# The first adaLN product moves from VectorE to TensorE in a hybrid decoder layer

## The chip, the cores and the metric

The kernel runs on one core of one Trainium2 chip. The metric is the device time of one execution, in microseconds (us). TensorE does the matrix products, VectorE (DVE in the rows) and ScalarE (ACT) the elementwise work, GpSimd (POOL) some more of it, and SyncE (SP) issues most transfers.

## The reference, cut to what matters

A decoder layer for 512 tokens of width 1024, one sequence. All data are fp32.

```python
c_act = silu(c)                                   # 1024 values
ada = c_act @ w_ada + b_ada                       # 1024 x 6144, split in six
sh_a, sc_a, g_a, sh_f, sc_f, g_f = split(ada, 6)
h = rmsnorm(x, norm_mix_w) * (1 + sc_a) + sh_a
proj = h @ w_in                                   # gq, gk, gv, gg, glr, hq, hf, hi, hg, ma, mb
log_alpha = log_sigmoid(glr @ w_gk2 + b_gk2) / 16 # glr has 16 columns
h_res = x + g_a * token_mixer(...)                # two gated linear attentions, merged, @ w_out
h = rmsnorm(h_res, norm_ffn_w) * (1 + sc_f) + sh_f
h_res = h_res + g_f * conv_ffn(h)                 # w_up, causal conv of 3, silu gate, w_down
out = rmsnorm(h_res, final_norm_w)
```

The change is about the first lines: `sh_a` and `sc_a` (columns 0 to 2047 of `w_ada`), `h`, and the 16 columns `glr`.

## The kernel before

The engines' programs are written out by hand, each engine has one list of instructions in order, and semaphores tie them together; there is no planner. Activations lie transposed in SBUF, features on partitions: eight tiles (KT = 8) of 128 x 512 tokens. Every large product is made of three products of split operands: `h_hi`, `h_lo` and `w_hi`, `w_lo` (the value rounded to a narrower fp32 form and the rest), so `three` (lines 1161 to 1168) issues hi x hi, lo x hi and hi x lo, each with 512 moving columns. Weights come as units of 128 columns x 1024 rows (512 KB) into three `raw` buffers; ScalarE makes `w_hi` (`split_hi`, L514), VectorE `w_lo` (`split_lo`, L785), in a ring of six slots.

The stages are: the start (about 0 to 38 us), the V stage (38 to 72 us), four groups of the mixer (to about 660 us with the output projection), the up and down products of the FFN, and the end. The change touches the first two.

The start. ScalarE issues the load of `x_tok` (L525); SyncE issues eleven small loads of vectors into `rows` (L326), then the weight unit 0, which holds the 16 low rank columns, and the first half of the ada weights in eight tiles with units 1 to 4 between them (L343, L351). TensorE turns `rows` (L1179) and then `x_tok` (L1186, 32 transposes in two halves; the second half waits until ScalarE and VectorE have copied the first out of PSUM as `xT`). ScalarE squares x (L534), VectorE and ScalarE make the inverse root (L851, L853, L541), VectorE spreads it over a diagonal (L860), TensorE sums that with ones (L1191), and ScalarE copies the result as `rb` (L546). GpSimd multiplies `xT` by `rb` into `xn` (L442).

The first ada product (L816, L819) is elementwise: for each tile k of 128 rows of `w_ada`, VectorE adds `ada_w0[k] * c_act[k]` to `ada_acc0` (128 x 1024), and TensorE then sums over partitions with eight products with a column of ones (`ada0_sums`, L1199). This happens in two halves q: half 0 serves the tiles k = 0 to 3 of h, half 1 the tiles 4 to 7. Half 1's eight VectorE steps stand between the `h_rest` steps (L838) in VectorE's list, after `rows_after` of 1, 2, 2 and 3. `ada0_finish` (L827, L830) adds the bias and forms the scale `a_mix`. ScalarE makes `h_hi` (L551) and the full `h_tmp` (L555) from `xn`, VectorE the rest `h_lo` (L838).

The V stage (the loop behind `ada0_sums(0)` in TensorE's list) runs over k = 0 to 7. For each k it does three products for the low rank unit into PSUM bank 2, and three for each of four token tiles t (the columns of units 1 to 4): 15 products per k, 120 in all. `ada0_sums(1)` stands at k = 3, before t = 1. After the stage come the low rank product z (L1289) and the further units, five microseconds or so each.

## Time and profile before

| what | us |
|---|---|
| median of the runs (lowest, highest) | 977.07 (976.78, 978.61) |
| span of the profiled execution | 976.7 |
| TensorE busy in it | 927.2 |
| VectorE busy | 544.0 |
| ScalarE busy | 466.6 |
| GpSimd busy | 179.8 |

The profiled execution's span is 0.4 us below the median of the runs. Times in a row are microseconds from the start of the span, durations in the group rows are busy microseconds and mean nanoseconds of one instruction, and PEld is TensorE's load of a stationary operand, which overlaps its products. The span was one stretch of TensorE work after a start of 38 us in which TensorE mostly waited.

### The profile page before, as it was taken

The numbers are of one execution on the slowest core, as the hardware profiler recorded it, in microseconds if no ns is written. First come the engines' busy times: TensorE is split into PE (matmuls) and PEld (weight loads), VectorE is DVE, ScalarE is ACT, GpSimd is POOL, SyncE is SP. The second block draws the span as 40 slices with busy tenths as digits, with TensorE's granted clock in tenths as the row PEclk, the third lists the DMA queues.
The fourth block names the chain that finished last, engine by engine and source line by source line (L and its number), as shares of the span: only waits on it lengthen the run. The fifth ranks groups of instructions, "written<-read, shape, count | busy, mean of one in ns | idle before, by whom it ended". The sixth has DMA issues, their size and how long they took to land.

```text
span 976.7 us, 13391 instructions
## 1 busy us (share of the span) xinstructions
PE 927.2 (95%) x4759; PEld 763.1 (78%) x4759; DVE 544.0 (56%) x674; ACT 466.6 (48%) x627; POOL 179.8 (18%) x115
## 2 busy tenths in 40 slices
PE   3699999999999999999999898999999999999995
PEld 2578888788887888878888776888888888888884
DVE  4846883567625677256773645664545454634317
ACT  5347664466634667356672743443333333523214
POOL 1501150311403114131041300021221122100002
PEclk9699999999999999999999999999999999999998
DMA  8915542454323543235422162243333333232202
GB/s 291 383 43 178 168 128 67 129 153 108 92 83 110 169 107 86 86 93 177 116 86 64 52 185 65 59 136 105 88 104 89 102 92 104 88 132 88 84 0 87
DMA packets 144238, 111.74 MB, mean 114 GB/s; under 512 B 3376, under 2 KB 131647, under 8 KB 143951
## 3 DMA queue, kind: packets, MB, share of 16 engines
q1 hardware_dynamic: 143647, 109.20, 36.7%
q10 hardware_dynamic: 528, 2.10, 0.6%
q8 instruction: 19, 0.31, 0.1%
q14 instruction: 12, 0.10, 0.0%
q0 software_dynamic: 32, 0.03, 0.0%
HBM read 107.13 MB, written 4.19 MB: 114 GB/s over the span
## 4 chain that ended last, share of the span: by engine, by line
PE 88%; DVE 5%; ACT 3%; issue 2%; DMA 1%; SPq 1%; DVEq 0%; ACTq 0%
PE ps L1165 27%; PE ps L1166 26%; PE ps L1167 26%; PE ps L1271 2%; DVE ada_acc L819 2%; PE ps L1256 2%; PE ps L1267 2%; DMA ada_w<-in_w_ada_dram 1%; DVE hres_tok L1146 1%; DVE w_lo L785 1%; PE ps L1281 1%; PE ps L1243 1%; PE ps L1199 1%; PE ps L1229 1%; ACT L595 1%
## 5 line engine op out<-in xcount | busy, mean ns | idle before, releaser
L1165 PE MATMUL ps<-h_hi,w_hi 128*128 128x512 f32 x872 | 348.4, 399 | 11.5 <-DVE h_lo L838 4.6
L1167 PE MATMUL ps<-h_hi,w_lo 128*128 128x512 f32 x872 | 341.2, 391 | 0.0
L1166 PE MATMUL ps<-h_lo,w_hi 128*128 128x512 f32 x872 | 341.0, 391 | 0.0
L785 DVE TENSOR_TENSOR w_lo<-raw,w_hi 128x1024 fp32r<-128x1024 f32 x147 | 200.0, 1366 | 91.9 <-ACT w_hi L514 91.5
L1165 PEld LDWEIGHTS ps<-h_hi,w_hi 128*128 128x128 f32 x872 | 164.6, 189 | 51.1 <-issue 14.2
L1167 PEld LDWEIGHTS ps<-h_hi,w_lo 128*128 128x128 f32 x872 | 164.6, 189 | 34.9
L1166 PEld LDWEIGHTS ps<-h_lo,w_hi 128*128 128x128 f32 x872 | 164.7, 189 | 34.3 <-issue 1.9
L514 ACT ACTIVATE w_hi<-raw 128x1024 fp32r<-128x1024 f32 x147 | 153.6, 1052 | 73.2 <-PE ps L1167 48.8
L1165 PE MATMUL ps<-w_hi,h_hi 128*128 128x512 f32 x296 | 116.8, 394 | 2.7 <-DVE w_lo L785 2.7
L1166 PE MATMUL ps<-w_lo,h_hi 128*128 128x512 f32 x296 | 116.0, 392 | 0.0
L1167 PE MATMUL ps<-w_hi,h_lo 128*128 128x512 f32 x296 | 115.9, 392 | 0.0
L721 ACT ACTIVATE conv<-ps,vecs 128x512 f32<-128x512 f32 x42 | 32.6, 778 | 130.6 <-PE ps L1167 130.6
L1096 DVE SCALAR_TENSOR_TENSOR conv<-ps,vecs,conv 128x511 f32<-128x511 f32 x44 | 33.0, 749 | 104.3 <-ACT conv L721 99.7
L496 POOL TENSOR_TENSOR prod<-conv 128x512 f32 x21 | 43.3, 2063 | 241.6 <-DVE conv L1100 241.6
L1165 PEld LDWEIGHTS ps<-w_hi,h_hi 128*128 128x128 f32 x296 | 56.1, 190 | 19.1 <-issue 5.1
L1166 PEld LDWEIGHTS ps<-w_lo,h_hi 128*128 128x128 f32 x296 | 56.1, 190 | 11.6
L1167 PEld LDWEIGHTS ps<-w_hi,h_lo 128*128 128x128 f32 x296 | 56.0, 189 | 11.7
L451 POOL TENSOR_TENSOR qs<-qs,qry 128x512 f32<-128x512 f32 x12 | 18.5, 1544 | 207.1 <-ACT qs L575 207.1
L949 DVE SCALAR_TENSOR_TENSOR ada_acc<-ada_w,cols,ada_acc 128x1024 f32<-128x1024 f32 x28 | 36.9, 1316 | 9.0 <-DMA ada_w<-in_w_ada_dram 8.9
L464 POOL TENSOR_TENSOR gate<-gate,oe 128x512 f32<-128x512 f32 x16 | 24.4, 1533 | 85.1 <-DVE oe L956 85.1
L641 ACT ACTIVATE gate<-ps 128x512 f32<-128x512 f32 x16 | 9.6, 597 | 61.8 <-PE ps L1167 61.7
L459 POOL TENSOR_TENSOR gate<-gate,gmul 128x512 f32<-128x512 f32 x16 | 24.4, 1523 | 79.1 <-ACT gmul L645 79.1
(183 smaller groups left out, 936.1 us busy)
## 6 DMA issues: line engine op xcount, KB each, us to landing
raw<-in_w_in_dram SPq DMA_DIRECT2D x73, 512.0 KB, 4.5
ada_w<-in_w_ada_dram SPq DMA_DIRECT2D x48, 512.0 KB, 5.0
...
x_tok<-in_x_dram ACTq DMA_DIRECT2D x1, 2048.0 KB, 8.4
xT_saved_dram<-xT SPq DMA_DIRECT2D x1, 2048.0 KB, 14.2
hres<-xT_saved_dram SPq DMA_DIRECT2D x1, 2048.0 KB, 7.9
```

The lines of the kernel that those rows point to most:

```text
L459: pool.tensor_tensor(gate[:, w], gate[:, w], gmul[:], ALU.mult).then_inc(gated, 1)
L464: pool.tensor_tensor(gate[:, w], gate[:, w], oe[:, w % 2], ALU.mult).then_inc(y_made, 1)
L496: pool.tensor_tensor(prod[:, bass.ds(r * 3 + q, 1), :].rearrange("p a t -> p (a t)"), conv[:, 2 * q], conv[:, 2 * q + 1], ALU.mult).then_i ...
L514: act.activation(w_hi[:, slot(u)].rearrange("p k c -> p (k c)"), raw[:, raw_slot(u)].rearrange("p k c -> p (k c)"), ACT.Copy).then_inc(hi_ ...
L721: act.activation(conv[:, m], ps[:, m], ACT.Identity, bias=vecs[:, bass.ds(ch + V_CONVB, 1)], scale=vecs[:, bass.ds(ch + V_TAP2, 1)]).then_ ...
L785: dve.tensor_tensor(w_lo[:, slot(u)].rearrange("p k c -> p (k c)"), raw[:, raw_slot(u)].rearrange("p k c -> p (k c)"), w_hi[:, slot(u)].re ...
L819: ins = dve.scalar_tensor_tensor(out=ada_acc0[:, q], in0=ada_w0[:, k], scalar=c_act[:, k:k + 1], in1=ada_acc0[:, q], op0=ALU.mult, op1=ALU ...
L949: ins = dve.scalar_tensor_tensor(out=ada_acc[:], in0=ada_w[:, m % 2], scalar=c_act[:, m:m + 1], in1=ada_acc[:], op0=ALU.mult, op1=ALU.add)
L1096: dve.scalar_tensor_tensor(out=conv[:, m, 1:T], in0=ps[:, m, 0:T - 1], scalar=vecs[:, bass.ds(ch + V_TAP1, 1)], in1=conv[:, m, 1:T], op0=A ...
L1165: pe.matmul(dst, a_hi, b_hi, start=start and i == 0, stop=False)
L1166: pe.matmul(dst, a_hi, b_lo, start=False, stop=False)
L1167: last = pe.matmul(dst, a_lo, b_hi, start=False, stop=stop and i == n - 1)
```

## The change

- The first ada product goes to TensorE. `c_act` is repeated 32 times (`c_rep`, 128 x 8 x 32) and is the stationary operand; blocks of 128 columns of `w_ada` are the moving one. The output of block j goes to partitions 32j to 32j + 31 of PSUM bank 7, so up to four blocks (two of shift, two of scale) are in the array at once, in four column groups. It is in plain fp32.
- The weights come in five pieces (`PIECES`: blocks 0-1, 2-3, 4-5, 6, 7, each for shift and scale) into two buffers. Piece 0 is summed before the V stage, pieces 1 to 4 inside it (`SUMS_AFTER`). ScalarE copies each sum out (`ada0_take`), TensorE transposes it into bank 3 (`ada0_turn`, `TURN_AFTER`), VectorE finishes it.
- The sixteen VectorE steps over `ada_w0` are gone. VectorE now makes `xs = xT * a_mix * rb` in one step per tile, and GpSimd's eight steps for `xn` are gone. ScalarE adds the shift, twice (`h_hi`, `h_full`); `h_full` has all eight tiles.
- The low rank projection leaves the list of split units (U_MIX is 0 instead of 1, so slots and counts move by one). GpSimd loads its 16 columns into a zeroed `w_lr` of 32 columns, and TensorE does eight fp32 products with 512 moving columns, in four column groups, just before k = 7, t = 0. The four partial sums stay on four groups of partitions, and z (L1289) sums them through a `gk2_g` that holds `w_gk2` four times.
- SyncE loads c and then x first. ScalarE issues the ten other vector loads. c is transposed apart from the rest.
- The waits for `xT_out` on ScalarE, VectorE and SyncE go; GpSimd's `merge` has one instead. Loads of the later ada pieces wait for `ada0_summed` on SyncE.

```diff
+PIECES = ((0, 2), (2, 2), (4, 2), (6, 1), (7, 1))
+PIECE_BUF = ((0, 0), (1, 0), (0, 0), (1, 0), (1, 1))
+SUMS_AFTER = {(0, 1): 1, (1, 2): 2, (3, 0): 3, (4, 0): 4}
+TURN_AFTER = {(0, 2): 1, (1, 3): 2, (3, 1): 3, (4, 1): 4}
+PIECE_OF = (0, 0, 1, 1, 2, 2, 3, 4)
...
-        ada_w0 = si("ada_w0", [P, KT, D])
-        ada_acc0 = si("ada_acc0", [P, 2, D])
-        h_tmp = si("h_tmp", [P, 2, T])
...
+        xs = si("xs", [P, 2, T])
+        ada_w0 = si("ada_w0", [P, 2, KT, 2, 2 * P])
+        ada_row = si("ada_row", [P, P])
+        h_full = si("h_full", [P, KT, T])
...
-            sp.wait_ge(rows_zero, 1)
-            def row(dst, src, n):
-                sp.dma_start(rows[dst % P:dst % P + n, dst // P, :], src).then_inc(rows_in, 16)
-            row(V_C, c[0].rearrange("(r p) -> r p", p=P), 8)
...
-            row(V_TAP2, conv_w[0, 2].rearrange("(r p) -> r p", p=P), 44)
...
+            sp.dma_start(c_row[:], c[0].rearrange("(r p) -> r p", p=P)).then_inc(c_in, 16)
+            sp.dma_start(x_tok[:], x[0].rearrange("(t p) d -> p t d", p=P)).then_inc(x_in, 16)
+
+            def ada0_load(i):
+                (k0, nb), (b, half) = PIECES[i], PIECE_BUF[i]
+                for a in range(2):
+                    sp.dma_start(ada_w0[:, b, :, a, half * P:(half + nb) * P],
+                                 wada_v[:, :, a * D + k0 * P:a * D + (k0 + nb) * P]).then_inc(ada0_in[i], 16)
...
             def first_load(u):
...
-            first_load(0)
-            for k in range(KT):
-                ada0_load(0, k)
-                if k % 2:
-                    first_load(k // 2 + 1)
-            for k in range(KT):
-                ada0_load(1, k)
+            ada0_load(0)
+            for u in range(RAW):
+                first_load(u)
+            ada0_load(1)
+            first_load(RAW)
+            sp.wait_ge(ada0_summed, 1)
+            ada0_load(2)
+            sp.wait_ge(ada0_summed, 2)
+            ada0_load(3)
+            ada0_load(4)
...
-                            sp.wait_ge(xT_out, 16)
                             sp.wait_ge(proj_done, 1)
...
+            pool.memset(w_lr[:], 0.0).then_inc(w_lr_zero, 1)
+            pool.memset(gk2[:], 0.0).then_inc(gk2_zero, 1)
+            pool.wait_ge(w_lr_zero, 1)
+            pool.dma_start(w_lr[:, :, 0:LOWRANK], win_v[:, :, GLR:GLR + LOWRANK]).then_inc(w_lr_in, 16)
+            pool.wait_ge(gk2_zero, 1)
+            for j in range(4):
+                pool.dma_start(gk2[32 * j:32 * j + LOWRANK, :], w_gk2[0]).then_inc(gk2_in, 16)
...
-            pool.wait_ge(rb_made, 1)
-            pool.wait_ge(start_act, 6)
-            for k in range(KT):
-                pool.wait_ge(xT_made_dve if k % 2 else xT_made_act, k // 2 + 1)
-                pool.tensor_tensor(xn[:, k], xT[:, k], rb[:], ALU.mult).then_inc(xn_made, 1)
-
-            pool.wait_ge(xT_out, 16)
...
+            act.wait_ge(rows_zero, 1)
+            def row(dst, src, n):
+                act.dma_start(rows[dst % P:dst % P + n, dst // P, :], src).then_inc(rows_in, 16)
+            row(V_BADA, b_ada[0].rearrange("(r p) -> r p", p=P), 48)
...
+            row(V_TAP2, conv_w[0, 2].rearrange("(r p) -> r p", p=P), 44)
...
-            act.activation(c_act, vecs[:, V_C:V_C + 8], ACT.Sigmoid).then_inc(start_act, 1)
+            act.wait_ge(c_turned, 1)
+            act.activation(c_act, ps[:, 1, 0:KT], ACT.Sigmoid).then_inc(start_act, 1)
...
+                if t:
+                    act.wait_ge(start_act, t + 2)
+                act.activation(x_sq[:], x_tok[:, t], ACT.Square, accum_out=ssq[:, t:t + 1]).then_inc(start_act, 1)
             for k in range(0, KT, 2):
                 act.wait_ge(x_turned, k + 1)
                 act.activation(xT[:, k], ps[:, 2 + k % 4], ACT.Copy).then_inc(xT_made_act, 1)
-            split_hi(0, 16, None)
             act.wait_ge(start_dve, 8)
             act.activation(rst[:, :], rst[:, :], ACT.Sqrt).then_inc(start_act, 1)
-            for u in range(1, U_MIX + AHEAD):
-                split_hi(u, 16 * raw_count(u), None)
-                if u == 3:
-                    act.wait_ge(rb_done, 1)
-                    act.activation(rb[:], ps[:, 6], ACT.Copy).then_inc(rb_made, 1)
-
+            split_hi(0, 16, None)
...
+            def ada0_take(i):
+
+                n = 2 * PIECES[i][1] * 32
+                act.wait_ge(ada0_summed, i + 1)
+                act.wait_ge(ada0_turned, i)
+                act.activation(ada_row[0:n], ps[0:n, 7, 0:P], ACT.Copy).then_inc(ada0_row_made, 1)
+
+            ada0_take(0)
+            split_hi(2, 16, None)
+            split_hi(3, 32, None)
             for k in range(KT):
-                act.wait_ge(ada0_made, 2 + 2 * (k // 4))
-                act.wait_ge(xn_made, k + 1)
-                act.activation(h_hi[:, k], xn[:, k], ACT.Identity, bias=ada[:, k:k + 1],
-                               scale=a_mix[:, k:k + 1]).then_inc(h_hi_made, 1)
-                if k >= 2:
-                    act.wait_ge(h_lo_made, k - 1)
-                act.activation(h_tmp[:, k % 2], xn[:, k], ACT.Identity, bias=ada[:, k:k + 1],
-                               scale=a_mix[:, k:k + 1]).then_inc(h_tmp_made, 1)
+                act.wait_ge(xs_made, k + 1)
+                act.activation(h_hi[:, k], xs[:, k % 2], ACT.Identity, bias=ada[:, k:k + 1]).then_inc(h_hi_made, 1)
+                act.activation(h_full[:, k], xs[:, k % 2], ACT.Identity, bias=ada[:, k:k + 1]
+                               ).then_inc(h_full_made, 1)
+                if k in (1, 3, 5, 6):
+                    ada0_take(PIECE_OF[k] + 1)
...
-            act.wait_ge(proj_done, 1)
-            act.activation(lrT[:, :], ps[0:LOWRANK, B_MISC], ACT.Copy).then_inc(taken_act, 1)
+            act.wait_ge(lr_done, 1)
+            act.activation(lrT[:, :], ps[:, B_MISC], ACT.Copy).then_inc(lr_taken, 1)
...
+            dve.wait_ge(start_act, 2)
+            dve.tensor_tensor(c_act, ps[:, 1, 0:KT], c_act, ALU.mult).then_inc(start_dve, 1)
+            dve.wait_ge(start_dve, 1)
+            dve.tensor_copy(c_rep[:], c_act.unsqueeze(2).to_broadcast([P, KT, 32])).then_inc(c_rep_made, 1)
...
+            def ada0_finish(i):
+
+                k0, nb = PIECES[i]
+                n = 2 * nb * 32
+                def part(ap):
+                    return ap.rearrange("p (a b) -> p a b", b=KT)[:, :, k0:k0 + nb]
+                dve.wait_ge(ada0_turned, i + 1)
+                dve.tensor_tensor(part(ada[:, 0:16]),
+                                  ps[:, 3, 0:n].rearrange("p (a b c) -> p a b c", b=nb, c=32)[:, :, :, 0],
+                                  part(vecs[:, V_BADA:V_BADA + 16]), ALU.add).then_inc(ada0_made, 1)
+                dve.wait_ge(ada0_made, 2 * i + 1)
...
+            def x_scaled(k):
+
+                if k >= 2:
+                    dve.wait_ge(h_full_made, k - 1)
+                dve.scalar_tensor_tensor(out=xs[:, k % 2], in0=xT[:, k], scalar=a_mix[:, k:k + 1], in1=rb[:],
+                                         op0=ALU.mult, op1=ALU.mult).then_inc(xs_made, 1)
...
-                dve.wait_ge(h_tmp_made, k + 1)
-                dve.tensor_tensor(h_lo[:, k], h_tmp[:, k % 2], h_hi[:, k].bitcast(F32), ALU.subtract
+                dve.wait_ge(h_full_made, k + 1)
+                dve.tensor_tensor(h_lo[:, k], h_full[:, k], h_hi[:, k].bitcast(F32), ALU.subtract
...
+            for j in range(1, KT, 2):
+                dve.wait_ge(x_turned, j + 1)
+                dve.tensor_copy(xT[:, j], ps[:, 2 + j % 4]).then_inc(xT_made_dve, 1)
+            dve.wait_ge(start_act, 6)
+            dve.tensor_scalar(rst, ssq, 1.0 / D, EPS, ALU.mult, ALU.add).then_inc(start_dve, 1)
+            dve.wait_ge(start_dve, 7)
+            dve.reciprocal(rst, rst).then_inc(start_dve, 1)
+            dve.wait_ge(start_act, 7)
+            for t in range(TT):
+                dve.tensor_scalar(rdiag[:, t * P:(t + 1) * P], ident[:], rst[:, t:t + 1], None,
+                                  ALU.mult).then_inc(rdiag_made, 1)
+            for u in range(3):
+                split_lo(u, u + 1)
+            ada0_finish(0)
+            dve.wait_ge(rb_made, 1)
+            dve.wait_ge(xT_made_act, KT // 2)
+            dve.wait_ge(xT_made_dve, KT // 2)
+            x_scaled(0)
+            x_scaled(1)
+            split_lo(3, 4)
...
             for k in range(KT):
...
                 h_rest(k)
...
+                if k in (1, 3, 5, 6):
+                    i = PIECE_OF[k] + 1
+                    ada0_finish(i)
+                    for j in range(*(PIECES[i][0], sum(PIECES[i]))):
+                        x_scaled(j)
...
-                dve.tensor_copy(gk2[0:LOWRANK, 0:P], gk2[32:32 + LOWRANK, bass.ds(g * P, P)]).then_inc(gk2_made, 1)
+                dve.tensor_copy(gk2_g[:], gk2[:, bass.ds(g * P, P)]).then_inc(gk2_made, 1)
                 if first:
-                    dve.wait_ge(xT_out, 16)
                     dve.wait_ge(mask_made, 6)
...
             pe.wait_ge(const_made, 3)
+            pe.wait_ge(c_in, 16)
+            pe.transpose(ps[:, 1, 0:KT], c_row[:], ident[0:KT, 0:KT]).then_inc(c_turned, 1)
+            pe.wait_ge(rows_in, 16 * 10)
...
+            def ada0_sums(i):
+
+                (k0, nb), (b, half) = PIECES[i], PIECE_BUF[i]
+                pe.wait_ge(ada0_in[i], 32)
+                pe.wait_ge(ada0_row_made, i)
+                for k in range(KT):
+                    for j in range(2 * nb):
+                        a, c0 = j // nb, (half + j % nb) * P
+                        last = pe.matmul(ps[32 * j:32 * j + 32, 7, 0:P], c_rep[:, k], ada_w0[:, b, k, a, c0:c0 + P],
+                                         start=k == 0, stop=k == KT - 1)
+                last.then_inc(ada0_summed, 1)
+
+            def ada0_turn(i):
+
+                n = 2 * PIECES[i][1] * 32
+                pe.wait_ge(ada0_row_made, i + 1)
+                pe.wait_ge(ada0_made, 2 * i)
+                pe.transpose(ps[:, 3, 0:n], ada_row[0:n], ident[0:n, 0:n]).then_inc(ada0_turned, 1)
+
             pe.wait_ge(rdiag_made, TT)
             for t in range(TT):
-                last = pe.matmul(ps[:, 6, t * P:(t + 1) * P], ones[:], h_tmp[:, 1, t * P:(t + 1) * P],
+                last = pe.matmul(ps[:, 6, t * P:(t + 1) * P], ones[:], rdiag[:, t * P:(t + 1) * P],
                                  start=True, stop=True)
             last.then_inc(rb_done, 1)
...
+            pe.wait_ge(c_rep_made, 1)
             ada0_sums(0)
+            pe.wait_ge(xT_made_dve, KT // 2)
+            ada0_turn(0)
...
+            def low_rank_part(half):
+
+                for k in range(4 * half, 4 * half + 4):
+                    pe.wait_ge(h_full_made, k + 1)
+                    j = 32 * (k % 4)
+                    last = pe.matmul(ps[j:j + 32, B_MISC], w_lr[:, k], h_full[:, k], start=half == 0, stop=half == 1)
+                return last
...
+            pe.wait_ge(w_lr_in, 16)
...
             for k in range(KT):
                 pe.wait_ge(h_lo_made, k + 1)
-                last = three(ps[:, B_MISC], [((w_hi[:, slot(0), k], w_lo[:, slot(0), k]), (h_hi[:, k], h_lo[:, k]))],
-                             start=k == 0, stop=k == KT - 1)
-                if k == KT - 1:
...
                 for t in range(TT):
-                    if k == 3 and t == 1:
-                        ada0_sums(1)
+                    if k == KT - 1 and t == 0:
+                        low_rank_part(0)
+                        low_rank_part(1).then_inc(lr_done, 1)
                     tok = slice(t * P, (t + 1) * P)
                     last = three(ps[:, V_BANKS[t]].rearrange("p (a b) -> p a b", b=P),
                                  [((h_hi[:, k, tok], h_lo[:, k, tok]), (w_hi[:, 0:4, k], w_lo[:, 0:4, k]))],
                                  start=k == 0, stop=k == KT - 1)
                     if k == KT - 1:
                         last.then_inc(proj_done, 1)
+                    if (k, t) in SUMS_AFTER:
+                        ada0_sums(SUMS_AFTER[k, t])
+                    if (k, t) in TURN_AFTER:
+                        ada0_turn(TURN_AFTER[k, t])
...
+                pe.wait_ge(lr_taken, 1)
...
+                pe.matmul(ps[:, MISC_Z], gk2_g[:], lrT[:], start=True, stop=True).then_inc(z_done, 1)
```

## Rows read from the trace of the kernel before

**Rows 1.** The page: busy time by engine, and busy tenths and clock in forty slices.

```profile
PE 927.2 (95%) x4759; PEld 763.1 (78%) x4759; DVE 544.0 (56%) x674; ACT 466.6 (48%) x627; POOL 179.8 (18%) x115
...
PE   3699999999999999999999898999999999999995
...
PEclk9699999999999999999999999999999999999998
```

**Rows 2.** TensorE's waits from 0 to 120 us: total, times, longest.

```profile
PE ps L1179 <- DMA rows<-in_conv_w_dram: 10.0, 1, 10.0
PE ps L1191 <- DVE h_tmp L860: 8.0, 1, 8.0
PE ps L1165 <- DVE h_lo L838: 4.6, 2, 4.0
PE ps L1186 <- ACT xT L538: 2.8, 1, 2.8
PE ps L1199 <- DVE ada_acc L819: 1.6, 2, 1.1
```

**Rows 3.** The chain that ended last, 0 to 90 us: start, us, what.

```profile
53.79 1.96 PE ps L1199 x16
...
72.45 1.05 PE ps L1289 x2
```

**Rows 4.** The timeline of the start: start, us, engine, line.

```profile
11.79 1.04 ACT L534 ACTIVATE xn<-x_tok 128x1024 f32<-128x1024 f32 x1
...
16.57 3.57 PE L1186 MATMUL ps<-ident,x_tok 128*128 128x128 f32 x16 [2.79 <-ACT xT L538]
...
20.99 1.28 ACT L541 ACT_TABLE_LOAD   x1
...
27.20 0.87 DVE L860 TENSOR_SCALAR h_tmp<-ident,cols 128x128 f32<-128x128 f32 x4
...
38.26 0.77 PE L1165 MATMUL ps<-h_hi,w_hi 128*128 128x512 f32 x1 [3.98 <-DVE h_lo L838]
```

**Rows 5.** Groups by line and form from 0 to 38.3 us.

```profile
L819 DVE SCALAR_TENSOR_TENSOR ada_acc<-ada_w,cols,ada_acc 128x1024 f32<-128x1024 f32 x7 | 9.0, 1280 | 1.0 <-DMA ada_w<-in_w_ada_dram 0.9
...
L785 DVE TENSOR_TENSOR w_lo<-raw,w_hi 128x1024 fp32r<-128x1024 f32 x5 | 6.7, 1334 | 0.4 <-ACT w_hi L514 0.4
...
L514 ACT ACTIVATE w_hi<-raw 128x1024 fp32r<-128x1024 f32 x5 | 5.1, 1049 | 2.5 <-DMA raw<-in_w_in_dram 2.5
...
L847 DVE COPY xT<-ps 128x512 f32<-128x512 f32 x4 | 2.7, 685 | 0.0
...
L551 ACT ACTIVATE h_hi<-xn,ada,cols 128x512 fp32r<-128x512 f32 x3 | 2.4, 803 | 3.0 <-DVE cols L830 3.0
...
L1191 PE MATMUL ps<-h_tmp,ones 128*128 128x128 f32 x8 | 2.1, 441 | 8.0 <-DVE h_tmp L860 8.0
```

**Rows 6.** Two stretches: length, PE, PEld, DVE, ACT, POOL busy, clock, DMA share, GB/s.

```profile
20.00:22.00 2.00, 0.15 (x2) 0.00 (x0) 1.97 (x5) 1.98 (x3) 0.00 (x0) 1.00 0.73 283
...
28.00:30.00 2.00, 1.87 (x8) 1.78 (x8) 1.90 (x3) 0.00 (x0) 0.00 (x0) 0.50 1.09 335
```

**Rows 7.** Two longer stretches, the same columns.

```profile
38.00:44.00 6.00, 5.74 (x14) 4.59 (x15) 5.90 (x5) 3.03 (x5) 6.00 (x4) 0.52 1.07 438
...
90.00:254.00 164.00, 163.11 (x989) 134.46 (x988) 111.17 (x136) 98.64 (x133) 39.88 (x25) 1.00 0.44 128
```

**Rows 8.** The chain around one `score` (L1243), 126 to 128 us.

```profile
126.42 0.58 PE ps L1243 x22
127.00 0.43 PE ps L1165
127.42 0.23 PE ps L1166
```

**Rows 9.** The instructions and shapes of one `score`, 95.8 to 96.6 us.

```profile
L1243 PE MATMUL ps<-qs,ks x32: 196/218/243, 95.9 to 96.3; 128*32 128x64 f32 x16, 128*32 128x32 f32 x16
```

**Rows 10.** The page, transfers: queue, count, KB, median us from issue to landing.

```profile
x_tok<-in_x_dram ACTq DMA_DIRECT2D x1, 2048.0 KB, 8.4
```

More of the change, by code:

```diff
@@ L49 @@
 NU = len(UNITS)
-U_MIX = 1
+U_MIX = 0
 U_OUT = U_MIX + GROUPS * NU
@@ L61 @@
 B_PROJ, B_MISC, B_STATE, B_O = 0, 2, 4, 6
-V_BANKS = (1, 0, 4, 5)
+V_BANKS = (0, 1, 4, 5)
 OUT_BANKS = (0, 1, 4, 5)
@@ L134, in build @@
         lbt = sb("lbt", [P, 5, KT])
-        lrT = sb("lrT", [LOWRANK, T])
-        gk2 = sb("gk2", [32 + LOWRANK, T])
+        lrT = sb("lrT", [P, T])
+        gk2 = sb("gk2", [P, T])
+        gk2_g = sb("gk2_g", [P, P])
         scan_mask = sb("scan_mask", [P, T], BF16)
@@ L142, in build @@
         si = sbuf(init)
+        xT = si("xT", [P, KT, T])
         rows = si("rows", [P, 3, P])
+        c_row = si("c_row", [KT, P])
+        c_rep = si("c_rep", [P, KT, 32])
+        w_lr = si("w_lr", [P, KT, 32])
         x_tok = si("x_tok", [P, TT, D])
-        xn = si("xn", [P, KT, T])
-        xT = si("xT", [P, KT, T])
-        ada_w0 = si("ada_w0", [P, KT, D])
-        ada_acc0 = si("ada_acc0", [P, 2, D])
-        h_tmp = si("h_tmp", [P, 2, T])
+        x_sq = si("x_sq", [P, D])
+        rdiag = si("rdiag", [P, T])
+        xs = si("xs", [P, 2, T])
+        ada_w0 = si("ada_w0", [P, 2, KT, 2, 2 * P])
+        ada_row = si("ada_row", [P, P])
+        h_full = si("h_full", [P, KT, T])
         rb = si("rb", [P, T])
@@ L202, in build @@
         fw_in = sem("fw_in")
-        ada0_in = [sem(f"ada0_in{i}") for i in range(KT)]
+        c_in = sem("c_in")
+        w_lr_in = sem("w_lr_in")
+        ada0_in = [sem(f"ada0_in{i}") for i in range(len(PIECES))]
         ada_in = [sem(f"ada_in{i}") for i in range(2)]
@@ L372, in group_loads @@
                     u = U_MIX + n
-                    if not (first and u < 5):
+                    if not (first and u < AHEAD):
                         load(u, win_v[:, :, bass.ds(g * step + c0, P)], g * NU + u - RAW + 1)
@@ L466, in merge @@
             def merge(g, w):
+                pool.wait_ge(xT_out, 16)
                 pool.wait_ge(y_made, g * 4 + w + 1)
@@ new lines, in _ @@
+            act.wait_ge(rb_done, 1)
+            act.activation(rb[:], ps[:, 6], ACT.Copy).then_inc(rb_made, 1)
+            split_hi(1, 16, None)
+            def ada0_take(i):
[6 more added lines that the diff above has]
+            split_hi(3, 32, None)
@@ L597, in root @@
                 act.activation(rn[:], rn[:], ACT.Exp, scale=-0.5).then_inc(rn_made, 1)
-            act.wait_ge(xT_out, 16)
             def group(g, first):
@@ L615, in group @@
                         exps(g, 2, 1.0)
-                    act.wait_ge(proj_done, g * NU + n + 2)
+                    act.wait_ge(proj_done, g * NU + U_MIX + n + 1)
                     bank = ps[:, V_BANKS[n] if first and n < 4 else B_PROJ + (U_MIX + n) % 2]
@@ L823, in ada0_finish @@
-            def ada0_finish(q):
-                def half(ap):
-                    return ap.rearrange("p (a b) -> p a b", b=8)[:, :, 4 * q:4 * q + 4]
-                dve.wait_ge(ada0_summed, q + 1)
-                dve.tensor_tensor(half(ada[:, 0:16]), ps[:, 7, 8 * q:8 * q + 8].rearrange("p (a b) -> p a b", b=4),
-                                  half(vecs[:, V_BADA:V_BADA + 16]), ALU.add).then_inc(ada0_made, 1)
-                dve.wait_ge(ada0_made, 2 * q + 1)
-                dve.scalar_tensor_tensor(out=a_mix[:, 4 * q:4 * q + 4], in0=ada[:, 8 + 4 * q:12 + 4 * q], scalar=1.0,
-                                         in1=vecs[:, V_NMIX + 4 * q:V_NMIX + 4 * q + 4],
-                                         op0=ALU.add, op1=ALU.mult).then_inc(ada0_made, 1)
-                dve.wait_ge(ada0_made, 2 * q + 2)
+            def ada0_finish(i):
[8 more added lines that the diff above has]
+                dve.wait_ge(ada0_made, 2 * i + 1)
+                dve.scalar_tensor_tensor(out=a_mix[:, k0:k0 + nb], in0=ada[:, 8 + k0:8 + k0 + nb], scalar=1.0,
+                                         in1=vecs[:, V_NMIX + k0:V_NMIX + k0 + nb],
+                                         op0=ALU.add, op1=ALU.mult).then_inc(ada0_made, 1)
+                dve.wait_ge(ada0_made, 2 * i + 2)
@@ L862, in _ @@
-            split_lo(3, 4)
-            split_lo(4, 5)
-            ada0_finish(0)
-            rows_after = (1, 2, 2, 3)
-            done = 0
-            for k in range(4):
-                h_rest(k)
-                for _ in range(rows_after[k]):
-                    ada0_rows(1, done)
-                    done += 1
-            ada0_finish(1)
-            for k in range(4, KT):
-                h_rest(k)
+            for j in range(1, KT, 2):
+                dve.wait_ge(x_turned, j + 1)
+                dve.tensor_copy(xT[:, j], ps[:, 2 + j % 4]).then_inc(xT_made_dve, 1)
```

107 lines of the change are left out of this document (32 added, 75 removed).

## The prediction

> **What bounds the kernel now.** I read the page first. TensorE is busy for 95% of the span, and the slices in which it clearly is not are the first two and the last [rows 1]. From 90 to 254 us it is busy for 163.1 of 164 us at the full clock [rows 7]. So in what follows the V stage nothing but TensorE counts, and a time saved ahead of it comes off the end one for one. The other engines are half idle, so an engine relieved is worth nothing by itself. The change lies wholly in the first 72 us.
>
> There I read the waits of TensorE [rows 2]. It waits 10.0 us for the vector loads, 2.8 for ScalarE's copy of `xT`, 8.0 for VectorE's diagonal, 0.5 for the first ada half, and 4.0 for the first `h_lo`. Then the timeline [rows 4] gives the order: ScalarE squares from 11.79, the second half of the transposes runs from 16.57 for 3.57 us, the table for the root is loaded at 20.99, the diagonal is made only at 27.20 and the V stage begins at 38.26. Between 20 and 28 us VectorE does ada steps of 1.28 us and `w_lo` steps of 1.3 us, in its fixed order, ahead of the diagonal [rows 5]. Last the chain: the second ada half is summed at 53.79 for 1.96 us, inside the V stage, and z begins at 72.45 [rows 3]. So the V stage takes 72.45 - 38.26 = 34.2 us. I call the two ends S (38.26 before) and V (72.45 before). The prediction is where V goes.
>
> **The start, up to S.**
> - x is issued behind c on SyncE, some 0.45 us later than now, and its 8.4 us to land [rows 10] give 0.8 + 0.45 + 8.4 = 9.7 us. Its bandwidth is not shared with the ada weights before, which were queued behind the vectors; I take it as unchanged. The vectors go on ScalarE's queue from the same 1.4 us as now, one fewer; they land at about 9.5 to 10.0, as before [rows 2], so the x transposes start when they do now, give or take 0.5.
> - The squares need only x and the early c: 9.8 instead of 11.79 [rows 4]. Each step now waits for the one before (one buffer `x_sq`), so I price it at 1.04 plus 0.2 (an estimate for the handover): four end at 14.7. First copy of `xT` 0.6, second half of the transposes 3.6 [rows 4]: 18.9. VectorE has no ada steps now and copies the last tile at once, 0.7 [rows 5]: 19.6. Two short steps and the root, about 0.6 (estimate; the table load of 1.28 [rows 4] runs from 18.6 beside them): 20.2. Diagonal 0.87 [rows 4]: 21.1. Before this point came at 28.1.
> - The sum of the diagonal takes 2.1 us at the low clock (1.2 GHz) [rows 5, 6] and, with half, 1.05 at the high one (2.4 GHz). Which? Transposes that ended at about 20.1 left the clock at 1.00 from 20 to 22, and 8 us later it was 0.50 [rows 6]. Here the gap is only 21.1 - 18.9 = 2.2 us. I take the high clock: 22.2. The low one is a rival.
> - `ada0_sums(0)`: 32 fp32 products of 128 columns. z shows two records of 512 columns in 1.05 us [rows 3]; taking 0.2 off for its start, a record costs 0.43, so a product of 128 columns (two records) costs 0.21. In turn, 32 cost 6.8 us; four column groups at once, 1.7. The nearest row is `score`: 32 records, 16 of 64 and 16 of 32 columns [rows 9], that in turn would cost 16 x 0.053 + 16 x 0.027 = 1.28 us and took 0.58 [rows 8], 2.2 times less. Its busiest column group alone has 8 x 0.053 = 0.43 us, so 0.15 is all that is left for loads and entry. That speaks for nearly full overlap, so I take 2.2 us, between 1.7 and 1.28/0.58's 3.1. End: 24.4. Piece 0 has long landed: x, piece 0 and three units are some 5.8 MB, 15 us at 390 GB/s, a value between the 335 of [rows 6] and the 438 of [rows 7].
> - ScalarE's copy of the sums and the turn, 0.35 each (estimate, a quarter of the 0.8 steps plus handover): 25.1. Now `split_hi(2)` stands behind the copy on ScalarE, 1.05, and VectorE does `split_lo(2)`, 1.22, before `ada0_finish(0)` [rows 5]: 27.4. Finish 0.4, two `xs` steps 1.4 (half of the 1.28 step each), `split_lo(3)` 1.22, `h_lo` 0.7, handovers 0.3: S = 31.4. ScalarE has `split_hi(3)` and both h steps (0.8 each [rows 5]) done beside that. The added waits on ScalarE (`rb_done`, the copy of the sums) hold units 1, 2 and 3 behind them; their price is in this chain.
> - GpSimd's multiplications are gone from the path; they hid behind VectorE before, so that is worth nothing but their slot. Its new loads (columns of `w_lr`, four of `w_gk2`) must land before S: the w_lr load has 1024 runs of 64 bytes, but over 20 us to do it; nothing.
>
> **The V stage.** What goes: 24 products of the low rank unit at 0.23 [rows 8], 5.5 us; `ada0_sums(1)`, 1.96 [rows 3]; the waits round it, 1.6 - 0.5 = 1.1 and 4.6 - 4.0 = 0.6 [rows 2]. 34.2 - 9.2 = 25.0 us for the 96 products that stay, in which the first 5.7 us run at the low clock (0.52 [rows 7]) at about 0.43 a product. I leave that penalty as it is, since TensorE has 6 idle us ahead of S.
> What comes, all on TensorE's path:
> - Pieces 1 and 2: 32 products each, 2.2 each. Pieces 3 and 4: 16 products in only two column groups, at least 8 x 0.21 = 1.7 each; I take 1.9. Sum 8.2. The first full product behind a column tiled run took 0.43 against 0.23 [rows 8]: 4 x 0.2 = 0.8.
> - Low rank: 8 products of 512 columns, 0.86 each: 6.9 in turn, 1.7 at four groups, 3.1 by the ratio of `score`. I take 2.1, plus 0.2.
> - Turns 0.4, and 0.3 for waits on the copies.
> That is 25.0 + 9.0 + 2.3 + 0.7 = 37.0 us, so V = 31.4 + 37.0 = 68.4. The stage itself is 2.8 us longer, and the start 6.9 shorter.
>
> A rule of the Trainium skill (TensorEngine Tiling (Array Packing), Key Properties) speaks against the change: going from one tiling mode to another drains the array. The trace agrees with a price, the 0.2 us of [rows 8]; were the entry to cost as much again, the six runs would add 1.2 us.
>
> Does the feed keep up? Per tile ScalarE needs 2 x 0.8 and VectorE 0.7 + 0.7, TensorE 12 x 0.23 = 2.8. A piece costs from its turn to its second `h_lo` about 0.4 + 1.4 + 1.6 + 0.7 = 4 us, and the list leaves (0,3), k = 1 and the next sums between: 5 us and more. Piece 4 is turned after (4,1), and k = 7 comes 10 us later. Hidden, if the order of things holds. Transfers: piece 2 waits on SyncE for sums 0 (24.4), 2 MB at about 0.39 MB/us is there by 33, needed at 42. Pieces 3 and 4 wait for sums 1 (38), are there by 46, needed at 48 and 53. Behind them on SyncE stand the store of `xT` and units 4 to 6, needed from about 60; two times 2 MB and 1.5 MB take 15 us from 38. Hidden too, with 7 us to spare. Before, that store was issued at 32 us.
>
> **After V.** The same work in the same order; z costs the same 1.05. The waits on `xT_out` that go had been over by then. GpSimd's clearing of `sT` waits for `proj_done` 1, which is now the first V product's end instead of the low rank's; 0.5 us, and three more products cover it.
>
> **The sum.** 72.45 - 68.4 = 4.05 us less: span 976.7 - 4.05 = 972.6. The median of the runs is 0.4 above the span, so 973.0.
>
> **The rivals.**
> - A, the forecast: 973.0; with full overlap (1.7 for each of the sums and for low rank) and S at 31.1, V = 31.1 + 25.0 + 7.6 + 1.9 + 0.4 = 66.0, which is 970.6. If TensorE comes to the high clock sooner, up to 1 us less. 60%.
> - B, overlap as the bare ratio of `score`: sums 3.1, 3.1, 1.8, 1.8, low rank 3.3, S 0.9 later. V = 32.3 + 25.0 + 10.6 + 3.3 + 0.7 = 71.9: 976.5, no change. For it: the row itself. Against it: two short and two long groups, which can't balance. The Trainium skill (TensorE: Matmul & The Clock Gate, Part 3) states 2.38 times for three column tiles of 512 columns; low rank would by that cost 2.9 us. 17%.
> - C, slower, by one mechanism: the two records of an fp32 product lie in one column group, and if the second must wait for the first and later products wait in line behind it, only two products overlap. Sums 3.4 for pieces 1 and 2, low rank 4.0, and on a low clock `ada0_sums(0)` 6.8. S = 31.4 + 1.05 + 4.6 = 37.0, V = 37.0 + 25.0 + 11.2 + 4.0 + 0.7 = 77.9: 982.5. It decides from the point where sums and low rank together cost over 4 us more than in A. Against it: `score` would take 0.64 us so, and took 0.58. 8%.
> - D, the clock is low from the diagonal on, or unit 3 (which waits behind piece 1 on the queue, due at about 27) lands after 29: S = 31.4 + 1.05 + 1.8 = 34.2, V = 71.2: 975.8. For it: the low clock at 28 us in [rows 6]. Against: the short gap. 12%.
> - E, no overlap at all (the change doesn't do what it says): sums 6.8, 6.8, 3.4, 3.4, low rank 6.9, S 4.6 later: V = 36 + 25.0 + 21.2 + 7.1 + 0.7 = 90: 994.5. `score` speaks against it. 3%.
>
> **How the numbers follow.** A measurement of this kernel can tell about 0.2%, 2 us, from no change: below 975.1 is faster, above 979.0 slower. A gives nearly all of faster, B and D a little of it: 66%. Same, B and D for the most: 20%. Slower, C and E and a few hundredths of the others: 14%. The range goes from 969.5 (A's end, clock sooner) to 979.0, between D and C, and leaves out most of C and E.
>
> **What would show it.** S near 31.4 and z near 68.4 in the chain; the diagonal's sum at 21 us at a clock of 1.00; 64 records of the sums in about 2.2 us; eight fp32 products of 512 columns in about 2.1; no wait of TensorE for `h_lo` over 0.5 us after S. The forecast fails if the sums of four groups take 3 us or more, if the clock is at 0.5 from 21 to 26 us, or if TensorE waits for a piece inside the stage.

## The result and the profile after

| what | before | after |
|---|---|---|
| median of the runs | 977.27 | 970.98 (969.41 to 971.61) |
| span of the profiled execution | 976.7 | 969.9 |
| V stage begins (S) | 38.26 | 33.39 |
| z begins (V) | 72.45 | 68.74 |

The ratio of the runs is 0.9932 (95% interval 0.992 to 0.9944): 6.3 us faster, where 4.1 were forecast. The page of the changed kernel, lines of busy time and clock, against [rows 1]:

```profile
PE 923.8 (95%) x4981; PEld 759.2 (78%) x4981; DVE 526.1 (54%) x672; ACT 465.7 (48%) x631; POOL 170.1 (18%) x113
...
PEclk9799999999999999999999999999999999999998
```

TensorE's waits from 0 to 120 us in the changed kernel (total, times, longest), against [rows 2]:

```profile
PE ps L1202 <- DMA rows<-in_conv_w_dram: 9.7, 1, 9.7
PE ps L1186 <- DVE h_lo L867: 8.3, 1, 8.3
PE ps L1233 <- DVE rdiag L879: 2.7, 1, 2.7
PE ps L1199 <- DMA c_row<-in_c_dram: 2.4, 1, 2.4
```

The 8.0 us before the diagonal became 2.7, but the wait for the first `h_lo` grew from 4.0 to 8.3. Inside the V stage there is no wait left. The timeline of the start (start, us, engine, line), against [rows 4]:

```profile
11.40 1.06 ACT L559 ACTIVATE x_sq<-x_tok 128x1024 f32<-128x1024 f32 x1 [4.07 <-DMA x_tok<-in_x_dram]
12.35 0.50 PEld L1202 LDWEIGHTS ps<-ident,rows 128*128 128x128 f32 x3 [9.83 <-DMA rows<-in_conv_w_dram]
...
20.35 0.87 DVE L879 TENSOR_SCALAR rdiag<-ident,cols 128x128 f32<-128x128 f32 x4 [0.73 <-ACT cols L565]
...
27.17 1.41 DVE L861 SCALAR_TENSOR_TENSOR xs<-xT,cols,rb 128x512 f32<-128x512 f32 x2
30.24 1.06 ACT L524 ACTIVATE w_hi<-raw 128x1024 fp32r<-128x1024 f32 x1 [4.63 <-DMA raw<-in_w_in_dram]
...
33.39 0.77 PE L1186 MATMUL ps<-w_hi,h_hi 128*128 128x512 f32 x1 [8.32 <-DVE h_lo L867]
```

The diagonal comes 6.9 us sooner (27.20 before). Then ScalarE waits 4.63 us for unit 3, whose load SyncE issued at 22.55, when the first `w_lo` had freed its buffer, and which landed 7.7 us later. That wait, not the arithmetic, sets S; e1 and e7 below test it. The chain through the V stage (start, us, what), against [rows 3]:

```profile
36.29 2.28 PE ps L1220 x64
...
42.33 1.88 PE ps L1220 x64
...
48.64 1.87 PE ps L1220 x32
...
53.88 1.87 PE ps L1220 x32
...
63.89 1.85 PE ps L1246 x16
65.75 0.43 PE ps L1186
...
68.74 0.86 PE ps L1334 x2
69.60 0.23 PE ps L1186
```

L1220 is the sums (64 records are 32 fp32 products), L1246 the low rank, L1334 z. The stage takes 68.74 - 33.39 = 35.35 us, 34.2 before.

Of the 6.8 us between the two profiled executions 3.7 have come when z begins. The rest comes later. The table cuts all profiled executions at the same places: S, the first z (V), the `h_lo` step that the chain shows ahead of the output product, the first `hres`, the `h_lo` ahead of the FFN, and VectorE's first step of the final norm. By it the mixer and its output product end at 569.0 us before, and the FFN begins at 601.4, not at about 660.

| kernel | S | V | mixer | output product | between | FFN |
|---|---|---|---|---|---|---|
| before | 38.26 | 72.45 | 471.20 | 25.38 | 32.37 | 355.67 |
| after | 33.39 | 68.74 | 469.71 | 23.77 | 32.38 | 355.66 |
| after, again | 33.27 | 69.43 | 469.66 | 25.22 | 32.37 | 355.63 |
| after, third | 33.65 | 69.75 | 469.70 | 25.21 | 32.37 | 355.72 |

The mixer is 1.5 us shorter in each, the output product 1.6 in one of three.

### The profile page after: what moved, and what is told of

Its sections match the earlier page's. It is cut to its first block, busy times and chain, and to the rows that moved or that the text cites. A ratio compares the mean times of both kernels' runs of the same rounds, so it can differ in the third digit from the quotient of the medians.

```text
span 969.9 us, 13833 instructions
## 1 busy us (share of the span) xinstructions
PE 923.8 (95%) x4981; PEld 759.2 (78%) x4981; DVE 526.1 (54%) x672; ACT 465.7 (48%) x631; POOL 170.1 (18%) x113
## 4 chain that ended last, share of the span: by engine, by line
PE 90%; ACT 3%; DVE 3%; DMA 1%; issue 1%; ACTq 0%; DVEq 0%
PE ps L1186 27%; PE ps L1188 26%; PE ps L1187 26%; PE ps L1316 2%; PE ps L1301 2%; PE ps L1312 2%; DVE w_lo L814 1%; DVE hres_tok L1167 1%; PE ps L1220 1%; PE ps L1326 1%; DMA raw<-in_w_in_dram 1%; PE ps L1288 1%; DMA rows<-in_conv_w_dram 1%; ACT w_hi L524 1%; PE ps L1274 1%
## 5 line engine op out<-in xcount | busy, mean ns | idle before, releaser
L1186 PE MATMUL ps<-h_hi,w_hi 128*128 128x512 f32 x864 | 344.5, 399 | 6.9 <-DVE h_lo L1105 3.3
L1188 PE MATMUL ps<-h_hi,w_lo 128*128 128x512 f32 x864 | 337.1, 390 | 0.0
L1187 PE MATMUL ps<-h_lo,w_hi 128*128 128x512 f32 x864 | 337.0, 390 | 0.0
L814 DVE TENSOR_TENSOR w_lo<-raw,w_hi 128x1024 fp32r<-128x1024 f32 x146 | 196.3, 1350 | 95.0 <-ACT w_hi L524 94.4
L1186 PEld LDWEIGHTS ps<-h_hi,w_hi 128*128 128x128 f32 x864 | 162.5, 188 | 44.9 <-issue 10.2
L1187 PEld LDWEIGHTS ps<-h_lo,w_hi 128*128 128x128 f32 x864 | 162.7, 188 | 34.4 <-issue 2.2
L1188 PEld LDWEIGHTS ps<-h_hi,w_lo 128*128 128x128 f32 x864 | 162.6, 188 | 34.3
L473 POOL TENSOR_TENSOR gate<-gate,oe 128x512 f32<-128x512 f32 x16 | 26.6, 1668 | 85.1 <-DVE oe L978 85.1
## 6 DMA issues: line engine op xcount, KB each, us to landing
x_tok<-in_x_dram SPq DMA_DIRECT2D x1, 2048.0 KB, 10.1
```

Source lines behind the costliest of these rows:

```text
L473: pool.tensor_tensor(gate[:, w], gate[:, w], oe[:, w % 2], ALU.mult).then_inc(y_made, 1)
L814: dve.tensor_tensor(w_lo[:, slot(u)].rearrange("p k c -> p (k c)"), raw[:, raw_slot(u)].rearrange("p k c -> p (k c)"), w_hi[:, slot(u)].re ...
L1186: pe.matmul(dst, a_hi, b_hi, start=start and i == 0, stop=False)
L1187: pe.matmul(dst, a_hi, b_lo, start=False, stop=False)
L1188: last = pe.matmul(dst, a_lo, b_hi, start=False, stop=stop and i == n - 1)
```

## The experiments

**The same kernel again (r1).** 

> The changed kernel once more, beside the others of this group. Both theories: 0.992 to 0.994 of before. Of the part behind the V stage: if the output product's stage got 1.6 us shorter by the phase of the clock alone, then its length (from the last h_lo of the mixer to the first hres) will be 23.8 us in some kernels of this study and 25.4 in others, whatever their edit; if it is a gain of the change, it will be 23.8 us in every kernel that has the change and 25.4 in every one that has not.

970.63 us, ratio 0.9922 (0.991 to 0.9935). The output product's stage took 25.22 us, as before the change. The stretches of the kernel before, then those of the first execution of the changed one, then those of this execution (length, PE, PEld, DVE, ACT, POOL busy, clock, DMA share, GB/s):

```profile
542.00:546.00 4.00, 1.44 (x4) 0.63 (x3) 3.89 (x4) 3.99 (x8) 3.72 (x3) 0.95 0.00 0
546.00:550.00 4.00, 4.00 (x13) 3.13 (x12) 3.24 (x5) 3.94 (x5) 0.29 (x1) 0.63 0.00 0
```

```profile
537.00:541.00 4.00, 1.44 (x6) 0.81 (x5) 3.89 (x4) 3.99 (x8) 3.74 (x3) 1.00 0.00 0
541.00:545.00 4.00, 4.00 (x20) 3.29 (x19) 3.06 (x6) 3.94 (x6) 0.10 (x1) 1.00 0.00 0
```

```profile
540.00:544.00 4.00, 3.28 (x8) 2.65 (x9) 4.00 (x6) 3.95 (x7) 1.72 (x2) 0.57 0.00 0
544.00:548.00 4.00, 4.00 (x19) 3.25 (x19) 2.78 (x4) 3.99 (x5) 1.30 (x1) 1.00 0.00 0
```

TensorE idles for the same 2.6 us in both executions of the changed kernel. In this one the clock falls (0.57), as it did before the change (0.63), in the other it stays at 1.00. So 1.6 of the 6.8 us between the two profiles are the clock's, and the changed kernel doesn't have them in every execution. Of the eleven profiled executions that hold the change, with or without a further edit, seven had 23.8 us here and four 25.1 to 25.3; the two without it (before, e3) had 25.4 and 25.5. Whether the change makes the short stage more frequent is not shown.

The clock also differed at the start. The first execution, then this one:

```profile
22.00:24.00 2.00, 2.00 (x64) 1.88 (x67) 0.52 (x1) 1.53 (x2) 0.00 (x0) 1.00 1.09 387
```

```profile
22.00:24.00 2.00, 2.00 (x23) 1.73 (x26) 0.65 (x1) 0.57 (x2) 0.00 (x0) 0.50 1.09 386
```

The diagonal's sum took 1.98 us and `ada0_sums(0)` 2.73 here, 1.16 and 1.95 in the first execution. S did not move (33.27), since unit 3 came at 30.1 all the same.

**A third time (r2).** 

> The changed kernel, a third time, for the comparison with the three below on the same chip. Its z began at 68.7 and 69.4 us in the two profiles so far; I expect it between 68.5 and 70 again, the spread being the granted clock in the sums of piece 1, and the stage of the output product at 23.8 or 25.4 us.

971.98 us; z at 69.75, output product 25.21, and the clock again low at 22 us (the diagonal's sum 1.68 us, `ada0_sums(0)` 3.03). The low clock lay across the sums of piece 1, which took 3.06 us here and 3.09 in the second execution, against 2.28 in the first.

**Unit 3 ahead of piece 1 (e1, and once more as r3).** 

> One edit on the changed kernel: unit 3 is queued ahead of ada piece 1. Theory T (the V stage begins when unit 3 has landed; its ScalarE split waited 4.6 us for it): unit 3 lands at about 26 instead of 30.2, the V stage begins at about 30.8 instead of 33.4, piece 1 lands at about 31 and is needed at 33.5, so the kernel is 2.6 us faster than the changed one. Rival (the transfers share one rate, and piece 1 then comes late by as much): the V stage begins sooner but TensorE waits 2 us or more for piece 1 or 2 inside it; no gain.

```diff
-            ada0_load(1)
             first_load(RAW)
+            ada0_load(1)
```

The timeline of this kernel:

```profile
28.10 1.06 ACT L524 ACTIVATE w_hi<-raw 128x1024 fp32r<-128x1024 f32 x1 [2.22 <-DMA raw<-in_w_in_dram]
31.25 0.77 PE L1186 MATMUL ps<-w_hi,h_hi 128*128 128x512 f32 x1 [5.92 <-DVE h_lo L867]
```

S moved from 33.39 to 31.25 and V from 68.74 to 66.19, with no wait inside the stage. That settles what set S in the changed kernel. But the five runs had a median of 971.37 us, no faster than the changed kernel's 970.63. So I ran it again.

> The kernel with unit 3 ahead of piece 1, once more: its z began 2.5 us sooner in the profile, but its runs had the same median as the changed kernel. Theory P (the gain at z is real, and the phase of TensorE's clock at the later gaps hides it in five runs): z at 66 to 67.5 again and, over both groups of runs, a mean 1 to 2.5 us below the changed kernel's. Rival (the one profiled run was a lucky one): z at 68 or later, no difference in the mean.

969.94 us, beside 971.98 for the changed kernel; S at 32.37, V at 67.50. In this execution the clock fell during the diagonal's sum (0.50 from 22 to 24 us), and with unit 3 out of the way the slower `ada0_sums(0)` (2.97 instead of 1.95 us) did move S. In the second execution of the changed kernel it had fallen too, and S was 33.27 all the same: the late unit 3 had hidden it. Over both groups the mean of the runs is 970.6 (9) against 971.3 (15) for the changed kernel. The gain at V is shown twice. The 0.7 us between the means misses the 1 to 2.5 that I had expected; these runs don't resolve what the gain at V is worth end to end.

**Fillers ahead of the V stage (e4).** 

> The edit of e1, and six fp32 products of 512 columns on TensorE into a free bank behind the turn of piece 0, which fill its idle time before the V stage (their result is not used). Theory (the first 5 us of the V stage run at 1.2 GHz because TensorE idled before): they end at about 30.5, the V stage runs at a granted clock of 1.00 from its first product and is 2.4 us shorter; 5 us faster than the changed kernel. Rival (the low clock is tied to the time since the start, not to idleness, or the fillers delay the stage): clock at 0.5 all the same, or a start at 31.5 and later; e1's time or worse.

```diff
             ada0_turn(0)
+            pe.wait_ge(rb_made, 1)
+            for i in range(6):
+                pe.matmul(ps[:, 6], ones[:], rdiag[:], start=True, stop=True)
```

969.41 us. The clock was 1.00 from 20 us on, as the theory had it. V came at 65.61, only 0.6 before e1's, not the 2.4 expected. In e1 the low clock had covered only the six products ahead of the first sums: 2.9 us, here 1.6. So 1.3 us was all there was to gain, and of that 0.5 went to a wait of the sums of piece 1 for their data, and 0.1 to a later start:

```profile
33.50 0.75 PE L1220 MATMUL ps<-ada_w,c_rep 128*32 128x128 f32 x20 [0.50 <-DMA ada_w<-in_w_ada_dram]
```

**Unit 3 in a buffer of its own (e7).** 

> Unit 3 gets a buffer of its own (two tiles of h_full that are not in use yet), so SyncE queues it right behind unit 2 with no wait, and piece 1 behind it. Theory (V begins when the engines' chain is done once unit 3 is early, and it is early in e1 already): V stage begins at 31.3 as in e1, z at 66 to 67, no wait for a piece. Rival (with transfers earlier still the V stage begins sooner): 30.5 or less.

```diff
+        def raw_of(u):
+            if u == RAW:
+                return h_full[:, KT - 2:KT].rearrange("p a (b c) -> p (a b) c", c=P)
+            return raw[:, raw_slot(u)]
...
             def first_load(u):
-                if u >= RAW:
-                    sp.wait_ge(lo_made, u - RAW + 1)
...
-            for u in range(RAW):
+            for u in range(RAW + 1):
                 first_load(u)
             ada0_load(1)
-            first_load(RAW)
```

968.61 us, ratio 0.9900 (0.9886 to 0.9915). S at 30.45 and V at 65.51: the rival's number, not the theory's. In e1 unit 3 had still been 2.2 us late; here ScalarE waits for no unit (it splits unit 3 at 25.48), and the engines' own chain sets S.

**Both (e8): the own buffer and seven fillers.** 

> As e7, with seven fp32 products of 512 columns on TensorE ahead of the V stage, as in e4. In e4 the V stage ran at a clock of 1.00 from its start but TensorE waited 0.5 us and more for piece 1, which had been queued behind unit 3's wait. Here piece 1 lands at about 26: no such wait, z at 64.8 to 65.2, 1 us below e4's 65.6 and 4 us below the changed kernel's. If the clock is what it saves, z of e8 is the same in every profile, and 1.3 to 2.6 us below e7's. Rival: the fillers end late and hold the stage back, z as in e7.

The same stretch in e7 and then in e8:

```profile
30.00:32.00 2.00, 1.55 (x4) 1.30 (x5) 0.99 (x2) 0.49 (x1) 0.00 (x0) 0.50 1.09 385
32.00:34.00 2.00, 2.00 (x28) 1.24 (x30) 0.00 (x0) 0.00 (x0) 0.00 (x0) 0.61 0.75 266
```

```profile
30.00:32.00 2.00, 2.00 (x9) 1.22 (x7) 0.86 (x2) 0.36 (x1) 0.00 (x0) 1.00 1.09 386
32.00:34.00 2.00, 2.00 (x66) 1.69 (x64) 0.00 (x0) 0.00 (x0) 0.00 (x0) 1.00 0.71 250
```

V at 64.36, S at 30.36: no start lost, and the stage is 1.06 us shorter. V is 1.15 us before e7's, somewhat less than the 1.3 to 2.6 expected. 968.92 us, ratio 0.9899 (0.9883 to 0.9916), so in the runs e7 and e8 can't be told apart. Both have a lower median than the changed kernel; against its runs of the same group (0.9928, 0.9913 to 0.9944) the intervals just overlap.

**The order of blocks in the sums (e2).** 

> One edit on the changed kernel: in the sums of a piece the block j is the outer loop and k the inner one, so successive products lie in the same column group. Theory O (four groups overlap fully, and only because neighbours in the order lie in different groups): pieces 0, 1 and 2 take 6.8 us each instead of 1.9 to 2.3, pieces 3 and 4 3.4 instead of 1.9, together some 18 us slower than the changed kernel. Rival (TensorE reorders across groups whatever the order of the list, or the products are short for another reason): no more than 3 us slower.

```diff
-                for k in range(KT):
-                    for j in range(2 * nb):
+                for j in range(2 * nb):
+                    for k in range(KT):
```

985.96 us, ratio 1.0082 (1.0065 to 1.0099). The chain of this kernel:

```profile
22.74 7.43 PE ps L1220 x64
...
39.17 6.08 PE ps L1220 x64
...
49.01 5.88 PE ps L1220 x64
...
59.31 3.21 PE ps L1220 x32
...
65.89 3.20 PE ps L1220 x32
```

The same products with the same operands take 5.9 to 6.1 instead of 1.9 us, three times as long (piece 0's 7.43 lay partly at a low clock, 0.62 and 0.53 from 22 to 26 us). The overlap is real, and here it was there only when neighbours in the list lay in different column groups. The 15 us lost in the medians (13.3 between the profiles at z) are less than the 18 expected, since of the 5.5 us more in piece 0 only 2.9 reached S (36.28): in the changed kernel the wait for unit 3 had filled the rest, and here ScalarE does not wait for it.

**Low rank, one product of eight (e5).** 

> The changed kernel with seven of the eight low rank products left out (the projection is then not computed in full). The eight took 1.85 us in the trace. If four groups overlap, the one left takes 0.86 and the kernel is 1.0 us faster than the changed one; if they overlap less than the trace suggests, 3 us or more.

The product that was left took 0.97 us in the chain and the eight 1.85; from S to V it is 34.90 us against 36.16 and 36.10 in the two executions with a similar clock, of which 0.3 is a shorter low clock. So eight products, two in each of four column groups, cost twice one, which is full overlap of four. The median of 971.69 us doesn't show a difference this small.

**GpSimd scales x (e6).** 

> One part of the change undone: x is scaled by GpSimd (eight products of xT and rb, 1.7 us each) as before, ScalarE applies a_mix, and VectorE's eight xs steps are gone. Theory (moving this to VectorE bought little; the gain of the start comes from taking the sixteen ada steps off VectorE, so that the diagonal is made 7 us sooner): V stage begins within 0.7 us of the changed kernel's 33.4, time within 1 us of it. Rival (GpSimd beside VectorE slows VectorE's steps, as h_lo at 1.3 instead of 0.7 us suggests, and the feed of the V stage falls behind): TensorE waits for h_lo inside the stage, 2 us or more slower.

```diff
+            for k in range(KT):
+                pool.wait_ge(xT_made_dve if k % 2 else xT_made_act, k // 2 + 1)
+                pool.tensor_tensor(xn[:, k], xT[:, k], rb[:], ALU.mult).then_inc(xs_made, 1)
...
-            x_scaled(0)
-            x_scaled(1)
```

The timeline:

```profile
24.66 12.01 POOL L460 TENSOR_TENSOR x_tok<-xT,rb 128x512 f32<-128x512 f32 x7
...
31.60 2.26 DVE L824 TENSOR_TENSOR w_lo<-raw,w_hi 128x1024 fp32r<-128x1024 f32 x1 [2.48 <-ACT w_hi L532]
...
33.79 3.43 DVE L870 TENSOR_TENSOR h_lo<-h_full,h_hi 128x512 fp32r<-128x512 f32 x2
35.68 0.76 PE L1185 MATMUL ps<-w_hi,h_hi 128*128 128x512 f32 x1 [10.36 <-DVE h_lo L870]
```

My theory missed. Unit 3 was there at 30.4 as in the changed kernel, but beside GpSimd `w_lo` takes 2.26 us instead of 1.23, `h_lo` 1.7 instead of 0.7, and S is 35.68, 2.3 us later. In the same execution `h_lo` is back at 0.69 us at 44.69, when GpSimd is done. Of the rival half is right: the steps slow down, but TensorE waits nowhere inside the stage. 972.45 us, ratio 0.9941 (0.9924 to 0.9958); the mean of its seven runs is 1.9 us above the mean of the changed kernel's 15, at intervals that overlap.

**Only z on 128 rows, in the kernel before (e3).** 

> The kernel before with one part of the change: z (the low rank product of each group) is made from 128 rows, of which 112 are zeroed, instead of 16. Theory Z (z on 16 rows switches the array's shape and back, and the change gave 0.4 us per group by not doing so): z takes 0.86 instead of 1.05 us, the first product behind it 0.23 instead of 0.43, four times: 1.6 us faster than before. Rival (z is shorter for another reason, such as its place or its operands): unchanged to 0.3 us.

```diff
-                pe.matmul(ps[:, MISC_Z], gk2[0:LOWRANK, 0:P], lrT[:], start=True, stop=True).then_inc(z_done, 1)
+                pe.matmul(ps[:, MISC_Z], gk2_g[:], lrT[:], start=True, stop=True).then_inc(z_done, 1)
```

Around the first z of the kernel before:

```profile
72.45 1.05 PE ps L1289 x2
73.50 0.43 PE ps L1165
73.93 0.23 PE ps L1166
```

In e3 every z took 0.86 us, and the mixer 468.85 us instead of 471.20: 2.35 less, of which 4 x 0.39 = 1.56 are z and the product behind it; the other 0.8 lie before the second z, where a wait of 0.9 us for `w_lo` wasn't there in this execution. The runs gave 976.82 us, ratio 0.9991 (0.9981 to 1.0002). So the trace bears the theory out; the time leans the same way and doesn't settle it.

## Why the prediction was right, and where it was not

The forecast was faster, 973.0 us; the result, 970.98 us, is faster and lies in the range. Point by point:

- **What bounds the kernel.** Right. Behind V every stage kept its length but for the items below.
- **The start.** S was forecast at 31.4 and came at 33.39. The step that failed is the landing of unit 3: I had it at about 27, after which ScalarE needs it, and named as rival D that it might land after 29. It landed at 30.2. That is D's condition, to which I gave 12% together with the low clock; and the low clock came too, in two of the three executions of the changed kernel, but hidden behind unit 3. Smaller terms were off and cancelled, which is luck: x took 10.1 us to land, not 8.4, and the vectors came at 12.35, not 10; but the clock stayed at 1.00 through both halves of the transposes, the second half took 2.0 us and not 3.6, and the diagonal came at 20.35 where I had 20.2. `ada0_sums(0)` took 1.95 us at the high clock (2.2), and 2.73 and 3.03 where the clock had fallen. e1 and e7 show the rest: with unit 3 early the V stage begins at 31.25 and 30.45, so the chain's sum was right to 1 us.
- **Which part of the change carries the start.** I had priced GpSimd's exit at nothing. e6 shows 2.3 us at S. The hint stood in the trace of before: with GpSimd busy `w_lo` took 1.82 us and `h_lo` 1.32 and 1.77, and 0.68 once GpSimd was done. How the gain of the start divides over the other parts of the change no run shows.
- **The V stage.** 37.0 us forecast, 35.35 to 36.2 measured. The sums took 2.28 to 3.09 for piece 1 (its share of the low clock), then 1.88, 1.87 and 1.87, for 2.2, 2.2, 1.9 and 1.9; low rank 1.85 for 2.1; the first full product behind each 0.43, as priced. No wait for a piece. Everything but the sums and low rank took 25.6 us in each of the three executions, where I had 26.7: I had left the low clock's 5.7 us whole on the full products, and here it covered six of them (0.43 each) and then part of the sums of piece 1. Rivals B, C and E fall: for groups that alternate the overlap is nearly full (1.88 us at the full clock, where full overlap would be 8 x 0.21 = 1.7), and e2 shows what no overlap costs. Two of my own signs of failure did show in r1 and r2, a clock of 0.50 from 22 us and sums of 3.0 to 3.1 us; the clock was their cause, since piece 2 took 1.89 in the same executions. The Trainium skill (TensorE: Matmul & The Clock Gate, Part 3) states 2.38 times for three tiles, by which low rank would be 2.9 us, an estimate; the four groups here gave 6.9 / 1.85 = 3.7, and no run here has three.
- **V.** 68.4 forecast, 68.7, 69.4 and 69.8 in three executions. It came out right by luck: I had the start 2.0 us too early and the stage 0.8 to 1.6 us too long.
- **After V.** "z costs the same" was wrong. z on 16 rows takes 1.05 us and makes the next product take 0.43; on 128 rows it takes 0.86 and the next 0.23. I had put the exit cost of a tiled run, 0.2 us, on the new products alone, and did not see that z was itself such a product, which the change makes a full one. The rule on draining in the Trainium skill (TensorEngine Tiling (Array Packing), Key Properties) says that a change of tiling mode drains the array; the 0.43 us of the product behind z agree with it, but it states no price. That is 1.5 us of gain that the sum lacked.
- **From the span to the median.** I added 0.4 us. All executions of this study show the run's time 1.7 to 1.9 us above its span, so the profiled execution of before was the slowest of its four runs (978.61), 1.3 us above their median. It had the long output product, the changed kernel's the short one.
- **The size of the gain.** What the change gives by the trace is 3.1 us at V (72.45 against the mean 69.3 of three) and 1.5 in the mixer, 4.6 us; e3, whose start is that of before, had z at 72.89. The means of the runs lie 6.5 to 6.9 us apart in the three groups in which both kernels ran. The 2 us between the two are open. Two things on record bear on them. Of the 15 runs of the changed kernel eleven took 969.4 to 971.6 us and four 973.3 to 974.1, and the executions profiled in r1 and r2 are two of those four, so the mean of three profiles leans to the longer ones. And the output product may be short more often with the change, worth 1.6 us each time; the FFN stage, 355.6 to 355.7 in all four executions of the table, was 1.6 us shorter in e4 and e8. One profile of each group can't say how often.
